# Two families of small products put into one stay on TensorE: the S5 outputs of a hybrid decoder layer

## The chip, the cores and the metric

The kernel runs on one core of a Trainium2 chip, in float32. The metric is the device time of one execution, in microseconds (us).

## What is computed

One layer of a decoder, for 256 prompt tokens and 8 samples of 4 tokens (288 tokens, 72 blocks of four). The mixer has two branches behind one large input projection; this case is about the end of the second, S5:

```python
u -> 128 groups of 16 channels, one 64-dim complex state per group
s_re, s_im = associative_scan(s5_combine, (a, b u)) + (a^t s0)      # per group
y = Re(C s) + d_skip * u
v = gelu(y) @ w_glu ; yB = v1 * sigmoid(v2)
merged = sigmoid(g_a) * yA + sigmoid(g_b) * yB
```

The kernel doesn't scan token by token. It takes blocks of four tokens: only the state at the start of each block is scanned (72 steps' worth of columns), and the four outputs of a block are the sum of

- the **Toeplitz products**: a 64 x 64 matrix for each group (4 tokens x 16 channels in, the same out; it holds C A^n B and the skip) times the block's inputs, for all 72 blocks at once, and
- the **state products**: a 64 x 64 matrix with the powers of A folded into C, once for the real and once for the imaginary part, times the states at the blocks' starts.

## The kernel before

**The stream.** TensorE works through 692 chunks of weights. A chunk is 128 x 1024 numbers in `raw`; ScalarE (ACT) rounds it to `w_hi`, VectorE (DVE) writes the remainder `w_lo`, and TensorE does 24 matmuls of 128 x 128 by 288 columns with it (`chunk`, L2092 to L2094: hi by hi, hi by lo, lo by hi). `raw`, `w_hi` and `w_lo` are rings of four chunks (`RING`), and the two roundings run three chunks ahead (`LEAD = 3`): in slot z of their programs ACT and DVE round the chunk of slot z + 3, for which ACT first waits until TensorE is through with slot z - 1. TensorE waits for `lo_ready` ahead of each chunk.

**The slots.** The stretch that matters is the loop over `SLOTS` = 84 chunks (chunk 240 + z is slot z), which all three engines have, written out by hand. Between the quarters (kt) of a chunk TensorE calls `s5_piece(z, kt)`, which puts small matmuls into the stream; each such interruption is a **stay** here. What stands where:

- slots 12 to 27 (`IN0`, `SCAN0`): matrices and inputs of the scan, among them the input products (`inputs`, L2365), 64 x 64 by 72 columns as well, on all four quarters of the array;
- slots 28 to 58 (`SCAN0` to `OUT0`): DVE runs the scan, two steps a slot (L1766, L1770, L1772), around its rounding;
- slots 38, 44, 50 and 56: the Toeplitz products of two blocks of 8 pairs of groups each (`t_products`, L2378). Pair p has two groups e = 0, 1; group e is read from partitions 64e and written to partitions 64e, so only two quarters of the array work. ACT lays the matrices out for them first (`t_block` into `tbd`) and copies the results over `u2` (`t_copy`);
- slots 59, 60, 62, 63, 65, 66, 68 and 69 (`out_slot`): the state products of one block each (`s5_out`, L2396), on four quarters. ACT copies the block's states ahead of them (`states_lay`, `states_lay_first`, into `so5`), DVE makes the matrices (`o_matrices`, into `qc` and `qc2` by turns, three operations for each of two parts) and adds the products to `u2` a slot later (`y_add`);
- `y_store` and `y_load` on GpSimd (POOL) move `u2` through a DRAM scratch, two blocks at a time, to the layout of features, and from slot 70 on `gelu_square`, `gelu_arg`, `gelu_tanh`, `gelu_out`, `v_round` and `v_remainder` make the operand of the GLU product, which begins in slot 84.

All of this waits on semaphores by count; several names share a semaphore (`SHARED`), and `reach` and `wait` add what the first user has left on it.

## Time and profile before

| | us |
|---|---|
| median of 3 runs | 2367.04 (2366.74 to 2367.44) |
| span of the profiled execution | 2365.0 |
| TensorE busy | 2358.0 (100%) |
| VectorE busy | 1654.1 (70%) |
| ScalarE busy | 1059.4 (45%) |
| Toeplitz products (L2378), 256 records in 4 stays | 8.9 |
| state products (L2396), 512 records in 8 stays | 9.8 |

The profiled execution's own time is its 2365.0 us span and some 2 us around it, by the median of the runs. The chain of waits that ended last is 99% TensorE. The trace shows a float32 matmul of the small kind as two records, each a load of 64 columns of weights and a pass of 72 columns, so 128 products are 256 records. Line numbers are those of the kernel before.

### The profile page before, as it was taken

To read this page: it belongs to the slowest core of one execution; us is meant where nothing else is said; L and a number is where in the kernel's file an instruction comes from. 1 tells how busy PE (TensorE), PEld (TensorE's weight loads), DVE (VectorE), ACT (ScalarE), POOL (GpSimd) and SP (SyncE) were. 2 spreads that over 40 slices of the span, in tenths; PEclk is the share of its full clock that TensorE was granted. 3 is DMA by queue.
4 is the path that set the end of the run, shared out by engine and by line. 5 is a ranking of instruction groups with operands and counts; after the bars stand their busy time and mean duration, and the time that the engine had idled before them with its cause. 6 is when DMAs were issued, how large, how long until landed. Compare 5 with 4: busy or idle time off the path is not lost.

```text
span 2365.0 us, 49376 instructions
## 1 busy us (share of the span) xinstructions
PE 2358.0 (100%) x19158; PEld 2305.6 (97%) x19158; DVE 1654.1 (70%) x2923; ACT 1059.4 (45%) x1567; POOL 109.2 (5%) x202
## 2 busy tenths in 40 slices
PE   9999999999999999999999999999999999999999
PEld 9999999999999999999999999999999999999998
DVE  7798988979888877798966655765555555544444
ACT  6553544535444445545643333553343334333333
POOL 1000000000000002100400000000000000000000
PEclk9999999999999999999999999999999999999999
DMA  7676766677676678465877766555655555565543
GB/s 213 203 226 203 239 197 207 215 214 237 187 222 204 219 236 232 146 185 166 249 203 199 203 194 201 178 169 158 174 161 161 170 161 165 169 200 165 169 159 117
DMA packets 546111, 453.93 MB, mean 192 GB/s; under 512 B 31184, under 2 KB 520112, under 8 KB 545408
## 3 DMA queue, kind: packets, MB, share of 16 engines
q1 hardware_dynamic: 525936, 406.23, 57.3%
q0 software_dynamic: 13392, 34.33, 4.5%
q10 hardware_dynamic: 6624, 11.18, 1.4%
q8 instruction: 109, 1.79, 0.3%
q14 instruction: 50, 0.41, 0.1%
HBM read 412.01 MB, written 38.81 MB: 191 GB/s over the span
## 4 chain that ended last, share of the span: by engine, by line
PE 99%; DVE 0%; issue 0%; ACT 0%; POOL 0%; POOLq 0%; DVEq 0%
PE acc L2092 31%; PE acc L2093 30%; PE acc L2094 30%; PE side L2079 1%; PE side L2178 1%; PE side L2230 1%; PE side L2365 0%; PE side L2102 0%; PE side L2396 0%; PE side L2378 0%; PE side L2211 0%; PE acc L2577 0%; PE side L2577 0%; PE side L2576 0%; PE acc L2576 0%; PE side L2575 0%
## 5 line engine op out<-in xcount | busy, mean ns | idle before, releaser
L1291 DVE TENSOR_TENSOR w_lo<-raw,w_hi 128x1024 fp32r<-128x1024 f32 (+2 forms) x692 | 831.0, 1208 | 508.2 <-ACT w_hi L792 503.1
L792 ACT ACTIVATE w_hi<-raw 128x1024 fp32r<-128x1024 f32 (+2 forms) x692 | 717.0, 1046 | 884.7 <-PE acc L2094 857.9
L2092 PE MATMUL acc<-h_hi,w_hi 128*128 128x288 f32 x3344 | 1000.9, 299 | 0.0
L2094 PE MATMUL acc<-h_hi,w_lo 128*128 128x288 f32 x3344 | 986.1, 295 | 0.0
L2093 PE MATMUL acc<-h_lo,w_hi 128*128 128x288 f32 x3344 | 985.2, 295 | 0.0
L2092 PEld LDWEIGHTS acc<-h_hi,w_hi 128*128 128x128 f32 x3344 | 627.9, 188 | 17.5 <-issue 15.1
L2093 PEld LDWEIGHTS acc<-h_lo,w_hi 128*128 128x128 f32 x3344 | 627.4, 188 | 2.2 <-issue 2.2
L2094 PEld LDWEIGHTS acc<-h_hi,w_lo 128*128 128x128 f32 x3344 | 627.8, 188 | 0.0
L2092 PE MATMUL acc<-f_hi,w_hi 128*128 128x288 f32 x698 | 207.0, 296 | 0.0
L2094 PE MATMUL acc<-f_hi,w_lo 128*128 128x288 f32 x698 | 205.7, 295 | 0.0
L2093 PE MATMUL acc<-f_lo,w_hi 128*128 128x288 f32 x698 | 205.4, 294 | 0.0
L2092 PE MATMUL acc<-y_hi,w_hi 128*128 128x288 f32 x512 | 155.4, 304 | 0.0
L2094 PE MATMUL acc<-v_hi,w_lo 128*128 128x288 f32 x512 | 151.8, 296 | 0.0
L2093 PE MATMUL acc<-v_lo,w_hi 128*128 128x288 f32 x512 | 151.6, 296 | 0.0
L2094 PE MATMUL acc<-y_hi,w_lo 128*128 128x288 f32 x512 | 150.9, 295 | 0.0
L2092 PE MATMUL acc<-v_hi,w_hi 128*128 128x288 f32 x512 | 150.9, 295 | 0.0
L2093 PE MATMUL acc<-y_lo,w_hi 128*128 128x288 f32 x512 | 150.7, 294 | 0.0
L2092 PEld LDWEIGHTS acc<-f_hi,w_hi 128*128 128x128 f32 x698 | 131.1, 188 | 0.0
L2094 PEld LDWEIGHTS acc<-f_hi,w_lo 128*128 128x128 f32 x698 | 131.0, 188 | 0.0
L2093 PEld LDWEIGHTS acc<-f_lo,w_hi 128*128 128x128 f32 x698 | 130.8, 187 | 0.0
L2092 PEld LDWEIGHTS acc<-y_hi,w_hi 128*128 128x128 f32 x512 | 96.2, 188 | 1.9 <-issue 1.7
L2093 PEld LDWEIGHTS acc<-y_lo,w_hi 128*128 128x128 f32 x512 | 96.1, 188 | 1.7 <-issue 1.7
(407 smaller groups left out, 2685.7 us busy)
## 6 DMA issues: line engine op xcount, KB each, us to landing
raw<-in_w_in_dram SPq DMA_DIRECT2D x512, 256.0 KB, 3.4
raw<-in_w_ffn_up_dram SPq DMA_DIRECT2D x352, 256.0 KB, 3.4
raw<-in_w_ffn_down_dram SPq DMA_DIRECT2D x160, 256.0 KB, 2.9
raw<-in_w_ssm_out_dram SPq DMA_DIRECT2D x128, 256.0 KB, 3.4
raw<-in_w_glu_dram SPq DMA_DIRECT2D x128, 256.0 KB, 3.7
h<-in_state_ssm_dram SPq DMA_DIRECT2D x32, 512.0 KB, 6.9
out_ssm_sample_dram<-h POOLq DMA_DIRECT2D x32, 512.0 KB, 3.8
raw<-in_w_out_dram SPq DMA_DIRECT2D x64, 256.0 KB, 3.2
```

The lines of the kernel that those rows point to most:

```text
L792: copy = lambda out, in_, **k: nc.scalar.activation(out, in_, ACT.Copy, **k)
L1291: tt(w_lo[:, slot, 0:n], raw[:, slot, 0:n], w_hi[:, slot, 0:n].bitcast(F32), ALU.subtract).then_inc(lo_ready, 1)
L2079: return pe.transpose(out, in_, ident[0:k, 0:k])
L2092: mm(o_, wh, xh[:, kt, :], start=first and i == 0, stop=False)
L2093: mm(o_, wh, xl[:, kt, :], start=False, stop=False)
L2094: done = mm(o_, wl, xh[:, kt, :], start=False, stop=last and i == n - 1)
L2178: last = mm(bank[r:r + 64, (j // 2) * n:(j // 2 + 1) * n], xdt[0:n, c, j * HD:(j + 1) * HD], abc[0:n, j, t0:t0 + n], **one)
L2230: last = mm(s3[32 * r:32 * r + 32, :], cm[:, b, :], h0[:, b, :], start=b < 4, stop=b >= 4)
```

## The change

The Toeplitz products leave slots 38 to 56. A stay now takes two blocks: first the Toeplitz products of both, which open the sums in the PSUM banks, then the state products of both, which add to them. There are four such stays, in slots 60, 64, 68 and 72 (`out_pair`), where there were four and eight. The Toeplitz matrix is read straight from `tt5`, whose layout is turned for it: its 64 columns now lie `PAIRS` x 4 = 256 bytes apart, where `tbd` had them side by side. Group e of pair 2r + g2 goes to half e ^ g2, so that all four quarters work.

`t_block`, `t_copy` and `y_add` are gone. ACT copies the finished sums to `u2` (`y_copy`, four copies in the slot behind a stay). `states_lay(1)` moves up to slot 59 and the later ones stand in the two slots behind a stay. There are three buffers for the state matrices (`qc3` is new); the matrices of block 2 are made in slots 48 and 51, within the scan, the others behind the stays. The rows of `u2` come out in reversed token order (`y_store` and, by the host's order of `w_glu`, the GLU product allow for that).

```diff
-def out_slot(i):
-
-    return OUT0 + i + i // 2
...
+def out_pair(z):
+
+    return (z - OUT0 - 1) // 4 if z in (OUT0 + 1, OUT0 + 5, OUT0 + 9, OUT0 + 13) else -1
...
-    tt5, at = sb("tt5", [P, DL, PAIRS, S5C], F32, used["u2"][1])
+    tt5, at = sb("tt5", [P, DL, S5C, PAIRS], F32, used["u2"][1])
...
-            def t_copy(i, h):
-
-                act.wait_ge(*reach("t_product", i * 2 + (h + 1)))
-                p0 = i * PB + 4 * h
-                copy(u2[:, p0:p0 + 4, :], ((s0, s1), (s2, s3))[i % 2][h][:, 0:4 * NK].rearrange("p (g k) -> p g k", k=NK)).then_inc(sem("t_copied"), 1)
+            def y_copy(i):
+
+                for g2 in range(2):
+                    act.wait_ge(sem("y5_product"), i * 2 + (g2 + 1))
+                    bank = ((s0, s1), (s2, s3))[i % 2][g2]
+                    v = u2[:, i * PB:i * PB + PB, :].rearrange("p (r g) k -> p g r k", g=2)[:, g2]
+                    copy(v, bank[:, 0:4 * NK].rearrange("p (g k) -> p g k", k=NK)).then_inc(sem("s5_y_copied"), 1)
...
                 if z == OUT0:
                     states_lay(0, 56)
-                if 0 <= out_block(z) < 7:
-                    states_lay(out_block(z) + 1)
+                    states_lay(1)
+                if out_pair(z - 1) >= 0:
+                    for i in (0, 1):
+                        y_copy(2 * out_pair(z - 1) + i)
+                if 0 <= out_pair(z - 1) < 3:
+                    states_lay(2 * out_pair(z - 1) + 2)
+                if 0 <= out_pair(z - 2) < 3:
+                    states_lay(2 * out_pair(z - 2) + 3)
...
-                if T0 <= z < T0 + 24:
-                    if (z - T0) % 3 == 1:
-                        t_block((z - T0) // 3)
-                    if (z - T0) % 6 == 5:
-                        for h in range(4):
-                            t_copy((z - T0) // 3 - 1 + h // 2, h % 2)
...
-                wait(dve, "y5_product", i * 2 - 2)
-                matrices(i, part, (qc, qc2)[i % 2], ct5, po5, ALU.add, ALU.subtract, "o")
-
-            def y_add(i):
-
-                dve.wait_ge(*reach("t_copied", i * 2 + 2))
...
+                if i == 2:
+                    dve.wait_ge(sem("p_product"), 16)
+                wait(dve, "y5_product", i * 2 - 4)
+                matrices(i, part, (qc, qc2, qc3)[i % 3], ct5, po5, ALU.add, ALU.subtract, "o", back=-1)
...
                 if z in (T0 + 6, T0 + 12):
                     o_matrices(1, (z - T0 - 6) // 6)
-                if out_block(z - 1) >= 0:
-                    i = out_block(z - 1)
-                    y_add(i)
-                    if i + 2 < 8:
-                        o_matrices(i + 2, 0)
-                        o_matrices(i + 2, 1)
+                if z in (T0 + 15, T0 + 18):
+                    o_matrices(2, (z - T0 - 15) // 3)
+                if out_pair(z - 1) >= 0 and 2 * out_pair(z - 1) + 3 < 8:
+                    for part in range(2):
+                        o_matrices(2 * out_pair(z - 1) + 3, part)
...
             def t_products(i):
 
-                if i == 0:
-                    pe.wait_ge(sem("p_copied"), 32)
-                pe.wait_ge(sem("tbd_ready"), i + 1)
-                wait(pe, "t_copied", i * 2 - 2)
-                for h in range(2):
-                    for p in range(4 * h, 4 * h + 4):
-                        for e in range(2):
-                            rows = slice(64 * e, 64 * e + 64)
-                            last = mm(((s0, s1), (s2, s3))[i % 2][h][rows, (p % 4) * NK:(p % 4 + 1) * NK], tbd[rows, i % 2, p, :], u2[rows, i * PB + p, :], **one)
-                    last.then_inc(sem("t_product"), 1)
...
+                banks = ((s0, s1), (s2, s3))[i % 2]
+                for r in range(4):
+                    for e in range(2):
+                        for g2 in range(2):
+                            rows, half = slice(64 * e, 64 * e + 64), 64 * (e ^ g2)
+                            pair = i * PB + 2 * r + g2
+                            last = mm(banks[g2][half:half + 64, r * NK:(r + 1) * NK], tt5[rows, :, :, pair].rearrange("p k c -> p (k c)"), u2[rows, pair, :],
+                               start=r == 0, stop=False)
+                last.then_inc(sem("t_product"), 1)
...
+            def s5_out(j):
+
+                if j == 0:
+                    pe.wait_ge(sem("p_copied"), 32)
+                    pe.wait_ge(sem("responses_shifted"), 96)
+                    pe.wait_ge(*reach("first_laid", 1))
+                pe.wait_ge(*reach("states_laid", 2 * j + 2))
+                pe.wait_ge(*reach("o_matrices", 4 * j + 4))
+                wait(pe, "s5_y_copied", 4 * j)
+                t_products(2 * j)
+                t_products(2 * j + 1)
+                state_products(2 * j)
+                state_products(2 * j + 1)
```

TensorE's order at its first stay behind the scan, which was in slot 59 (the last row is the beginning of slot 59's last quarter). Here is before:

```order
L2092 MATMUL acc<-h_hi,w_hi 128x288
L2093 MATMUL acc<-h_lo,w_hi 128x288
L2094 MATMUL acc<-h_hi,w_lo 128x288
L2396 MATMUL side<-so_108,qc 64x72 x32
L2092 MATMUL acc<-h_hi,w_hi 128x288
```

Of the changed kernel, the same place in slot 60, 24 rows of chunk work later; `tt_115` is `tt5`, `so_108` is `so5`, `qc_107` is `qc2`:

```order
L2081 MATMUL acc<-h_hi,w_lo 128x288
L2363 MATMUL side<-u_112,tt_115 64x72 x32
L2376 MATMUL side<-so_108,qc 64x72 x32
L2376 MATMUL side<-so_108,qc_107 64x72 x32
L2079 MATMUL acc<-h_hi,w_hi 128x288
```

The first stay has moved by one slot and holds three times as many products, all behind the waits that the state products have; the rows of L2378 in slots 38 to 56 are gone.

DVE's order within the scan, in slots 48 and 49 (`scr` and `st` are the scan's). Before:

```order
L1291 TENSOR_TENSOR w_lo<-raw,w_hi 128x1024
L1770 TENSOR_TENSOR scr_122<-scr_122 128x128
L1772 TENSOR_TENSOR st_120<-st_120,scr_122 128x128
L1766 TENSOR_TENSOR scr_122<-st_120,a4t 128x256
L1770 TENSOR_TENSOR scr_122<-scr_122 128x128
L1772 TENSOR_TENSOR st_120<-st_120,scr_122 128x128
L1766 TENSOR_TENSOR scr_122<-st_120,a4t 128x256
L1291 TENSOR_TENSOR w_lo<-raw,w_hi 128x1024
```

And of the changed kernel, where `qc_128` is `qc3`:

```order
L1283 TENSOR_TENSOR w_lo<-raw,w_hi 128x1024
L1755 TENSOR_TENSOR scr_122<-scr_122 128x128
L1757 TENSOR_TENSOR st_120<-st_120,scr_122 128x128
L1751 TENSOR_TENSOR scr_122<-st_120,a4t 128x256
L1755 TENSOR_TENSOR scr_122<-scr_122 128x128
L1757 TENSOR_TENSOR st_120<-st_120,scr_122 128x128
L1704 TENSOR_TENSOR tm_110<-ct_117,po_124 128x512
L1705 TENSOR_TENSOR tm_110<-ct_117,po_124 128x512
L1710 TENSOR_TENSOR qc_128<-tm_110 128x512
L1751 TENSOR_TENSOR scr_122<-st_120,a4t 128x256
L1283 TENSOR_TENSOR w_lo<-raw,w_hi 128x1024
```

One part of block 2's matrices, three operations, now stands between two steps of the scan, and the second part the same way in slot 51.

ACT's order around the end of the scan, from slot 58. Before:

```order
L792 ACTIVATE so_108<-st_120 128x16x56
L792 ACTIVATE w_hi<-raw 128x1024
L792 ACTIVATE so_108<-st_120 128x16x16
L792 ACTIVATE so_108<-st_120 128x1152
L792 ACTIVATE w_hi<-raw 128x1024
L792 ACTIVATE so_108<-st_120 128x1152
```

Of the changed kernel:

```order
L789 ACTIVATE so_108<-st_120 128x16x56
L789 ACTIVATE w_hi<-raw 128x1024
L789 ACTIVATE so_108<-st_120 128x16x16
L789 ACTIVATE so_108<-st_120 128x1152
L789 ACTIVATE w_hi<-raw 128x1024
L1001 ACTIVATE gth<-acc 128x288 x2
L1003 DMA mix_scratch<-gth 128x576
L789 ACTIVATE w_hi<-raw 128x1024
L789 ACTIVATE u_112<-side 128x4x72 x4
L789 ACTIVATE so_108<-st_120 128x1152
```

Up to slot 59 the same copies stand in the same order, but the first stay now waits for the second of slot 59's two, which is block 1's; the copy of block 2's states has gone behind the first stay's results.

## Rows read from the trace of the kernel before

**Rows 1.** The page's busy times: us (share of the span) x instructions.

```profile
PE 2358.0 (100%) x19158; PEld 2305.6 (97%) x19158; DVE 1654.1 (70%) x2923; ACT 1059.4 (45%) x1567; POOL 109.2 (5%) x202
```

**Rows 2.** TensorE by line and form: busy us, mean ns of one | idle before.

```profile
L2396 PE MATMUL side<-so,qc 64*64 64x72 f32 x512 | 9.8, 226 | 0.3 <-issue 0.3
```

**Rows 3.** Timeline, TensorE, first Toeplitz stay: start us, us, instruction.

```profile
1026.81 0.30 PE L2094 MATMUL acc<-h_hi,w_lo 128*128 128x288 f32 x1
1027.04 2.22 PE L2378 MATMUL side<-u,tbd 64*64 64x72 f32 x64
...
1029.42 0.30 PE L2093 MATMUL acc<-h_lo,w_hi 128*128 128x288 f32 x1
```

**Rows 4.** Timeline, TensorE, first state stay, next chunk, last state stay.

```profile
1104.70 0.30 PE L2094 MATMUL acc<-h_hi,w_lo 128*128 128x288 f32 x1
1104.92 1.23 PE L2396 MATMUL side<-so,qc 64*64 64x72 f32 x64
...
1106.32 0.30 PE L2093 MATMUL acc<-h_lo,w_hi 128*128 128x288 f32 x1
...
1106.99 0.29 PE L2092 MATMUL acc<-h_hi,w_hi 128*128 128x288 f32 x1
...
1146.64 1.23 PE L2396 MATMUL side<-so,qc 64*64 64x72 f32 x64 [0.28 <-issue]
```

**Rows 5.** Timeline, TensorE, one stay of input products.

```profile
941.49 0.98 PE L2365 MATMUL side<-u,pw 64*64 64x72 f32 x48
```

**Rows 6.** Windows, 90 us of the scan: PE, PEld, DVE, ACT, POOL busy (x records), clock.

```profile
1000.00:1090.00 90.00, 90.00 (x819) 89.27 (x818) 85.01 (x190) 42.52 (x82) 5.66 (x7) 1.00 0.61 182
```

**Rows 7.** Timeline, VectorE: roundings of slots 33, 38, 39, 40, 58; scan's end.

```profile
1013.10 1.22 DVE L1291 TENSOR_TENSOR w_lo<-raw,w_hi 128x1024 fp32r<-128x1024 f32 x1
...
1029.27 1.22 DVE L1291 TENSOR_TENSOR w_lo<-raw,w_hi 128x1024 fp32r<-128x1024 f32 x1
...
1033.04 1.23 DVE L1291 TENSOR_TENSOR w_lo<-raw,w_hi 128x1024 fp32r<-128x1024 f32 x1 [0.46 <-ACT w_hi L792]
...
1038.21 1.22 DVE L1291 TENSOR_TENSOR w_lo<-raw,w_hi 128x1024 fp32r<-128x1024 f32 x1
...
1100.66 1.22 DVE L1291 TENSOR_TENSOR w_lo<-raw,w_hi 128x1024 fp32r<-128x1024 f32 x1
...
1103.22 0.29 DVE L1772 TENSOR_TENSOR st<-st,scr 128x128 f32<-128x128 f32 x1
```

**Rows 8.** Timeline, ScalarE: roundings of slots 34, 35, 60; copies of states.

```profile
1013.66 1.06 ACT L792 ACTIVATE w_hi<-raw 128x1024 fp32r<-128x1024 f32 x1 [2.12 <-PE acc L2094]
...
1016.85 1.06 ACT L792 ACTIVATE w_hi<-raw 128x1024 fp32r<-128x1024 f32 x1 [1.33 <-PE acc L2094]
...
1103.66 2.83 ACT L792 ACTIVATE so<-st 128x256 f32<-128x256 f32 x2
1107.25 1.06 ACT L792 ACTIVATE w_hi<-raw 128x1024 fp32r<-128x1024 f32 x1 [0.75 <-PE acc L2094]
```

**Rows 9.** Windows, TensorE: window, us, busy (x records), granted clock, DMA.

```profile
2.00:4.00 2.00, 1.97 (x9) 1.00 0.90 250
6.00:8.00 2.00, 2.00 (x20) 1.00 1.03 430
...
2364.00:2365.00 1.00, 0.00 (x0) 0.59 0.15 50
```

**Rows 10.** Timeline, TensorE: its last matmuls.

```profile
2360.82 0.65 PE L2518 MATMUL side<-fW,ident 128*128 128x288 f32 x2
```

**Rows 11.** ScalarE by line and form, 985 to 1195 us: busy us, mean ns.

```profile
L792 ACT ACTIVATE w_hi<-raw 128x1024 fp32r<-128x1024 f32 x59 | 62.5, 1060 | 77.2 <-PE acc L2094 76.6 <-ACT gth L1004 0.5
L792 ACT ACTIVATE so<-st 128x1152 f32<-128x1152 f32 x7 | 16.2, 2315 | 0.0
```

**Rows 12.** Timeline, GpSimd: store and load of the last quarter of y.

```profile
1154.18 4.48 POOL L763 DMA_DIRECT2D y_scratch<-u  x8
...
1166.54 1.34 POOL L773 DMA_DIRECT2D yt<-y_scratch  x2 [0.83 <-issue]
```

More of the change, by code:

```diff
@@ L83 @@
 FIN0 = OUT0 + 17
-def out_slot(i):
-    return OUT0 + i + i // 2
-def out_block(z):
-    return {out_slot(i): i for i in range(8)}.get(z, -1)
+def out_pair(z):
+    return (z - OUT0 - 1) // 4 if z in (OUT0 + 1, OUT0 + 5, OUT0 + 9, OUT0 + 13) else -1
 def gelu_at(z):
@@ L312, in build @@
     yt5, _ = sb("yt5", [P, KT, T], F32, used["u2"][0])
-    gsq, at = sb("gsq", [P, 2, T], F32, used["tt5"][0])
-    gar, at = sb("gar", [P, 2, T], F32, at)
-    assert at <= used["tt5"][1]
+    gsq, at = sb("gsq", [P, 2, T], F32, used["qc3"][0])
+    assert at <= used["qc3"][1]
+    gar, at = sb("gar", [P, 2, T], F32, used["tm5"][0])
+    assert at <= used["tm5"][1]
     v_hi, at = sb("v_hi", [P, KT, T], F32R, used["st5"][0])
@@ L1703, in _, with matrices @@
                 s5_parameters(t)
-            def matrices(i, part, bd, src, pows, re_sub, im_rev, s, n=DL):
+            def matrices(i, part, bd, src, pows, re_sub, im_rev, s, n=DL, back=1):
                 block = slice(i * PB, i * PB + PB)
                 xr, xi = [bc(src[:, k, block, :], n, 2) for k in range(2)]
-                qr, qi = [bc(pows[:, k, 0:n, block].rearrange("x j p -> x p j"), S5C, 3) for k in range(2)]
+                qr, qi = [bc(pows[:, k, 0:n, block][:, ::back].rearrange("x j p -> x p j"), S5C, 3) for k in range(2)]
                 v = [tm5[:, k, 0:PB * n * S5C].rearrange("x (p j c) -> x p j c", p=PB, j=n) for k in range(2)]
@@ L1843, in _ @@
                     o_matrices(1, (z - T0 - 6) // 6)
-                if out_block(z - 1) >= 0:
-                    i = out_block(z - 1)
-                    y_add(i)
-                    if i + 2 < 8:
-                        o_matrices(i + 2, 0)
-                        o_matrices(i + 2, 1)
+                if z in (T0 + 15, T0 + 18):
[3 more added lines that the diff above has]
+                        o_matrices(2 * out_pair(z - 1) + 3, part)
+                for part in range(2):
+                    if out_pair(z - 2 - part) >= 0 and 2 * out_pair(z - 2 - part) + 4 < 8:
+                        o_matrices(2 * out_pair(z - 2 - part) + 4, part)
                 if gelu_at(z - 1) >= 0:
@@ L2415, in s5_piece @@
                         inputs(7, 1)
[L2416 to L2422 removed]
+                if out_pair(z) >= 0 and kt == 2:
+                    s5_out(out_pair(z))
             pe.wait_ge(sem("y_split"), 32)
@@ L2674 @@
     quarters = [2 * (i // 4) + i % 2 + 8 * (i % 4 // 2) for i in range(KT)]
-    given['w_glu'] = given['w_glu'].reshape(1, KT, P, 2 * D_MODEL)[:, quarters].reshape(1, D_MODEL, 2 * D_MODEL)
+    by_tile = given['w_glu'].reshape(1, KT, 4, 2, S5C, 2 * D_MODEL)[:, quarters]
+    by_tile = _np.stack([by_tile[:, i, :, ::-1] if i % 4 // 2 else by_tile[:, i] for i in range(KT)], axis=1)
+    given['w_glu'] = by_tile.reshape(1, D_MODEL, 2 * D_MODEL)
     arrays, a, o = {}, {}, {}
```

58 lines of the change are left out of this document (18 added, 40 removed).

## The prediction

> **What bounds the kernel now.** First the page's busy times: TensorE is busy for 2358.0 us of a 2365.0 us span [rows 1]. Then its waits: in 90 us of the stretch of this change there is none [rows 6], and among the small products one of 0.3 us [rows 2], ahead of the last state stay [rows 4]. So all that leaves TensorE is gained in full, as long as nobody else becomes late. That is the second question, and it goes to the engine whose share of the whole (70%) hides where it stands: in 90 us of the scan VectorE is busy for 85.01 [rows 6], and its timeline is a gapless row of short dependent operations. The pace of that row against the pace of TensorE decides this case.
>
> **What TensorE sheds.** A Toeplitz stay: from the last matmul ahead (1026.81) to the second behind (1029.42) are 2.61 us [rows 3]. Without a stay two matmul steps would lie there; 24 matmuls take 3.19 us (two roundings of ScalarE, each released by a finished chunk, are 3.19 apart [rows 8]), so a step is 0.133 and the stay costs 2.61 - 0.27 = 2.34. A state stay costs 1106.32 - 1104.70 = 1.62, less 0.27: 1.35 [rows 4]. Before: 4 x 2.34 + 8 x 1.35 = 20.2 us, and the 0.3 of waiting.
>
> After: 128 Toeplitz products (256 records) and 256 state products (512) in 4 stays, 192 records each. The pace of the state products: 64 records run 1.23 us to the end of the last, which itself takes 0.226 [rows 2], so (1.23 - 0.23) / 63 = 0.016 a record [rows 4]. The Toeplitz products of before, on two quarters: (2.22 - 0.22) / 63 = 0.032 [rows 3]. The input products, of the same size, on four quarters and in the same order of rows and halves as the new Toeplitz products: (0.98 - 0.22) / 47 = 0.016 [rows 5]. Four records in 0.064 us on four quarters, two in 0.064 on two: the quarters work side by side. I take 0.016 for the new Toeplitz products too, since the two rows nearest in form have it; the upper bounds follow with the rivals. A stay is then 1.35 + 128 x 0.016 = 3.40, four are 13.6. **TensorE sheds 20.2 + 0.3 - 13.6 = 6.9 us.** If nothing else moved, that would be the gain.
>
> **What VectorE gets in the scan.** Its period per slot is one rounding and two scan steps: from 1013.10 (slot 33) to 1029.27 (slot 38) are 5 periods of 3.234 us [rows 7]. TensorE's slot without a stay is 3.187 (24 steps). So VectorE is slower than TensorE by 0.047 us a slot all through the scan, and what let it keep up were the Toeplitz stays, 2.34 us each, in which TensorE stood aside. It shows: the first slot behind the first of them is where VectorE had to wait (0.46 at 1033.04 [rows 7]). The change takes all four away and adds work: one part of `o_matrices` stretches a period to 1038.21 - 1033.04 = 5.17, so it costs 1.94, and there are now four of them in the scan (slots 39, 45, 48, 51) where there were two.
>
> Nothing makes VectorE wait any more from slot 33 on, so slot 58 rounds at 1013.10 + 25 x 3.234 + 4 x 1.94 = 1101.7, and the scan ends as long behind it as before (1103.22 + 0.29 - 1100.66 = 2.85 [rows 7]): at **1104.6**. Before it was 1103.5, with 9.4 us of Toeplitz stays in TensorE's program to cover it.
>
> TensorE: a chunk begins 0.26 us ahead of the ScalarE rounding that it releases (1106.99 and 1107.25 [rows 4, 8]), so slot 34 begins at 1013.66 - 0.26 = 1013.40. Unhindered, slot 60 would begin 26 slots on, at 1096.3, and its three quarters would be through at 1098.7. Two waits stand against that:
>
> - The remainders. Chunk 52 is rounded in slot 49, at 1013.10 + 16 x 3.234 + 3 x 1.94 + 1.22 = 1071.9; TensorE wants it at 1013.40 + 18 x 3.187 = 1070.8. From there on VectorE sets the pace. Chunk 60 is ready at 1101.7 - 3.2 + 1.2 = 1099.7, so slot 60 begins 3.4 us late and comes to its stay at 1102.1.
> - The states. The stay in slot 60 wants block 0's and block 1's states, and the last of the scan goes into both. ScalarE copied them in 2.83 us from 0.15 after the scan's end [rows 7, 8]; after, that is 1104.6 + 2.98 = **1107.6**. TensorE stands for 5.5 us. In the queue behind ScalarE's wait are the roundings from slot 60 on, which TensorE doesn't want before slot 63. Before, TensorE needed only block 0's states at this point, a slot earlier, and came late enough.
>
> Together 8.9 us of new waits. In TensorE's time: the stay begins at 1107.6, is through at 1111.0; before, the same point of slot 60 was 1106.99 + 2.39 + 1.35 = 1110.7, so the change is 0.3 behind. Later stays: before 6 x 1.35 + 0.3 = 8.4, after 3 x 3.40 = 10.2, 1.8 more. **Net 2.0 us slower.**
>
> **The clock.** TensorE's last matmul ends at 2361.47 [rows 10], and in the last microsecond of the span the granted clock is 0.59 on average [rows 9]: it had fallen to the lower level, 1.2 GHz, by about 2364.2, 2.7 us after the last work. The new wait is twice as long, behind a dense stretch. At the kernel's start the records come at half pace, 9 in two microseconds against 20 from 6 us on [rows 9]: after a pause TensorE ran at the lower level for some 3.4 us of work. The same behind the first stay's wait costs half of that: 1.7 us. I count it in: 2.0 + 1.7 = **3.7 us slower**.
>
> **What costs nothing, and why.** Leaving: ScalarE's `t_block` and `t_copy` (it is busy for 42.52 of 90 us there [rows 6]). Coming: 16 `y_copy` in place of 16 copies of the same 288 columns, and two copies of states in the two slots behind each stay. Behind the first stay ScalarE has 1.06 + 4 x 0.4 + 2.3 = 5.0 us in a slot of 3.2 and 3.4 in the next [rows 11]; it falls 2 us behind and has them back before the next stay, whose states are then laid. The lead of the roundings is three slots, 9.6 us, less the 2.3 that the two take. VectorE loses eight `y_add` and gets the matrices over two or three slots each. The last two blocks are finished in slot 72, not 69: y is copied at about 1163, and store and load took 1166.54 + 1.34 + about 5 - 1154.18 = 19 us [rows 12], so it is there at 1182, against 1180.6 when ScalarE comes to it in slot 79. A wait of some 1.6 us, inside the lead; without that cover it would cost just this. `skip_added` and the copies into `tt5` keep their sizes; the latter fall in slots 13 to 27, where VectorE has idle time in every slot.
>
> **Rivals.**
>
> *Slower weight loads (the other side: clearly slower).* The new Toeplitz matrices are read at a step of 256 bytes. No row of TensorE has such a read. ScalarE has: 1152 states with a step of 512 bytes took 2315 ns, 2.01 each, 1024 weights side by side 1060, 1.04 each [rows 11]. If a load of 64 columns, which by its share of 64 in 64 + 72 columns takes 30 ns of the 64 that a quarter needs, takes twice as long, four records take 30 ns more: 7.5 x 256 = 1.9 us. If it takes ScalarE's 2.01 ns a column, 129 in place of 30: 99 / 4 x 256 = 6.3 us. Net 3.9 to 8.3 with the full clock, 5.6 to 10.0 with the fall. Against it speaks only that nothing says TensorE reads as ScalarE does. From 1.0 us on it would make the loss measurable.
>
> The Trainium skill has this as a rule (SBUF — State Buffer, "Specifications (TRN2)"): SBUF has lines of 16 bytes, full bandwidth needs at least two hits on a line, and each step to a new line pays. It gives no price, and read for TensorE it would make this rival the likeliest case. ScalarE's two rows [rows 11] agree with it; for TensorE no row shows it.
>
> *The clock stays up.* The 5.5 us are a sum of small terms, and the only fall in the trace came behind a sparse stretch. If this wait brings none, net 2.0: 2369.0.
>
> *The cover holds.* If VectorE's period shrinks when TensorE reads less, or the first stay's waits are already met, the 6.9 us are gained: 2360.1. Against it: the five periods of 3.234 include the first Toeplitz stay (1027.04 to 1029.2 [rows 3]), and the period at 1013.10 wasn't waiting for anything either.
>
> **How the numbers follow.** The profiled execution took its span of 2365.0 and some 2 us around it; I add to the median, 2367.04. Forecast: 2367.04 + 3.7 = 2370.7 us, chance 0.32. Clock stays up: 2369.0, 0.18. Slower loads: 2371 to 2377, 0.42, of which 0.34 lie over 2371.8. Gain: 2360.1, 0.05. The rest, 0.03, is scattered. 0.2% of the time, about what a measurement can tell from no change, is 4.7 us: faster 0.05, same 0.60, slower 0.35. The range leaves out the gain and the dearest loads with a fallen clock: 2368.0 to 2375.4.
>
> **What would show it.** Right: no L2378 stays, four stays in slots 60, 64, 68, 72; VectorE without a gap from slot 33 to the scan's end at about 1104.6; TensorE's chunks waiting for `w_lo` from slot 52 on, at most 2 us at once, then about 5.5 us ahead of the first stay; a granted clock under 1 behind it; a later stay of 3.4 us. A later stay of 3.9 to 5.0 means slow loads. No wait ahead of slot 60's stay would prove the argument on VectorE wrong, and so would a scan that ends before 1103.

## Result and profile after

The changed kernel took 2379.76 us (median of 4 runs, 2378.83 to 2383.74) beside 2367.16 us for the kernel before on the same chip (4 runs): ratio 1.0057, 95% interval 1.0045 to 1.0068. It is slower by 12.6 us. The forecast was 2370.7, its range ended at 2375.4, and the likeliest sign was "same". The profiled execution has a span of 2377.1 us against 2365.0.

The page of the kernel after, engines and the chain that ended last (compare [rows 1]; the chain was 99% TensorE, now VectorE is in it):

```profile
PE 2359.8 (99%) x19158; PEld 2308.7 (97%) x19158; DVE 1649.3 (69%) x2907; ACT 1050.4 (44%) x1535; POOL 109.2 (5%) x202
...
PE 95%; DVE 5%; issue 0%; ACT 0%; POOL 0%; POOLq 0%; ACTq 0%; DVEq 0%
```

TensorE's waits in 985 to 1210 us of the kernel after (engine, line, what it waited for: us in total, times, longest). In the same place before there was one of 0.3 [rows 4]:

```profile
PE side L2363 <- ACT so L789: 5.1, 1, 5.1
PE acc L2079 <- DVE w_lo L1283: 2.8, 2, 1.7
PE acc L2079 <- issue: 2.7, 1, 2.7
```

The first two are the waits of the prediction. The third, "issue", is time in which TensorE stood and no engine's work is shown as what it waited for. Nothing in the prediction answers to it.

The first stay (slot 60) in the timelines of VectorE, ScalarE and TensorE, and TensorE's granted clock around it (columns of the windows: length, busy time of PE, PEld, DVE, ACT and POOL with their instructions, clock, DMA share, GB/s):

```profile
1105.01 0.29 DVE L1757 TENSOR_TENSOR st<-st,scr 128x128 f32<-128x128 f32 x1
```

```profile
1105.34 2.70 ACT L789 ACTIVATE so<-st 128x256 f32<-128x256 f32 x2 [6.28 <-DVE st L1757]
```

```profile
1108.30 2.63 PE L2363 MATMUL side<-u,tt 64*64 64x72 f32 x64 [5.09 <-ACT so L789]
1110.63 3.61 PE L2376 MATMUL side<-so,qc 64*64 64x72 f32 x128
```

```profile
1106.00:1107.00 1.00, 0.00 (x0) 0.00 (x0) 0.44 (x1) 1.00 (x1) 0.00 (x0) 0.86 0.69 240
1107.00:1108.00 1.00, 0.00 (x0) 0.00 (x0) 0.00 (x0) 1.00 (x2) 0.00 (x0) 0.50 0.27 54
...
1113.00:1114.00 1.00, 1.00 (x57) 1.00 (x52) 0.00 (x0) 0.00 (x0) 0.00 (x0) 0.73 0.52 178
1114.00:1116.00 2.00, 2.00 (x30) 1.92 (x20) 0.00 (x0) 0.67 (x1) 0.00 (x0) 1.00 0.00 0
```

The scan ends at 1105.30 (on this trace, whose chunks already start 0.8 us later at the kernel's beginning), ScalarE copies the states, TensorE starts when they are there. Its clock falls to the lower level while it waits and is back at the higher one towards 1113.5; 128 records of the state products take 3.61 us here and 2.18 in a later stay.

The last stay (slot 72), with the chunk around it (compare [rows 3] and [rows 4]):

```profile
1161.78 0.29 PE L2081 MATMUL acc<-h_hi,w_lo 128*128 128x288 f32 x1
1162.01 2.58 PE L2363 MATMUL side<-u,tt 64*64 64x72 f32 x64
1164.40 2.18 PE L2376 MATMUL side<-so,qc 64*64 64x72 f32 x128
...
1166.75 0.29 PE L2080 MATMUL acc<-h_lo,w_hi 128*128 128x288 f32 x1
1166.88 0.29 PE L2081 MATMUL acc<-h_hi,w_lo 128*128 128x288 f32 x1
1169.84 0.40 PE L2079 MATMUL acc<-h_hi,w_hi 128*128 128x288 f32 x1 [2.66 <-issue]
```

Measured as in the prediction, a later stay costs 1166.75 - 1161.78 - 0.27 = 4.70 us, not 3.40. The state products run as forecast (128 records in some 2.2 us). The Toeplitz products don't: 64 records take 1164.40 - 1162.01 = 2.39 us, where 16 ns each would be 1.02. And 2.96 us, less one step of 0.13, are lost three matmuls behind the stay.

**The ledger.** Comparing the starts of all chunks in the two traces, slot by slot, gives the whole difference of the spans (12.1):

| | forecast, us | measured, us |
|---|---|---|
| start of the kernel, ahead of all chunks | 0 | +0.8 |
| stays of before gone (4 of 2.34, 8 of 1.35, wait 0.3) | -20.5 | -20.6 |
| four new stays at the full clock | +13.6 | +18.8 |
| waits for `w_lo`, slots 51 to 59 | +3.4 | +3.5 |
| wait for the states, slot 60 | +5.5 | +5.1 |
| lower clock in slot 60 | +1.7 | +1.5 |
| gap behind the last stay | 0 | +2.9 |
| sum | +3.7 | +12.0 |

Two rows are off: the stays by 5.2, and the gap. The runs go after both, and after what the waits are worth.

### The profile page after: what moved, and what is told of

The parts are those of the page before. It is cut to its first block, busy times and chain, and to the rows that moved or that the text cites. A ratio compares the mean times of both kernels' runs of the same rounds, so it can differ in the third digit from the quotient of the medians.

```text
span 2377.1 us, 49310 instructions
## 1 busy us (share of the span) xinstructions
PE 2359.8 (99%) x19158; PEld 2308.7 (97%) x19158; DVE 1649.3 (69%) x2907; ACT 1050.4 (44%) x1535; POOL 109.2 (5%) x202
## 4 chain that ended last, share of the span: by engine, by line
PE 95%; DVE 5%; issue 0%; ACT 0%; POOL 0%; POOLq 0%; ACTq 0%; DVEq 0%
PE acc L2079 29%; PE acc L2080 28%; PE acc L2081 28%; DVE w_lo L1283 1%; PE side L2066 1%; DVE scr L1751 1%; PE side L2165 1%; DVE st L1757 1%; DVE scr L1755 1%; PE side L2217 1%; PE side L2089 0%; PE side L2352 0%; PE side L2363 0%; PE side L2376 0%; PE side L2198 0%
```

## Experiments

### The step of the weights

Contiguous weights in an otherwise unchanged kernel. Only the address is changed, so that the Toeplitz products multiply by wrong numbers:

```diff
-                            last = mm(banks[g2][half:half + 64, r * NK:(r + 1) * NK], tt5[rows, :, :, pair].rearrange("p k c -> p (k c)"), u2[rows, pair, :],
+                            last = mm(banks[g2][half:half + 64, r * NK:(r + 1) * NK], tt5[rows, :, :, :].rearrange("p k c q -> p (k c q)")[:, pair * 64:pair * 64 + 64], u2[rows, pair, :],
```

> The changed kernel, but the Toeplitz products read 64 weights side by side (columns 64p to 64p + 63 of tt5) in place of 64 at a step of 256 bytes; these are other numbers, so y is not the layer's. Theory (the step makes the loads slow): a record of the Toeplitz products takes 16 ns in place of 36, a stay 3.4 us in place of 4.7, the kernel 4 x 1.3 = 5.2 us less, about 2374.5. Rival (both row halves of the array write into one bank): pace stays 36 ns, time stays 2379.8. Open: whether the 2.7 us without an instruction, seen in the last slot of stays, stays.

Measured: 2378.57 us (5 runs, 2374.78 to 2380.97), 1.0043 (1.0029 to 1.0058). TensorE's last stay in the timeline:

```profile
1158.26 1.23 PE L2363 MATMUL side<-u,tt 64*64 64x72 f32 x64
1159.31 2.18 PE L2376 MATMUL side<-so,qc 64*64 64x72 f32 x128
...
1167.64 0.61 PE L2079 MATMUL acc<-h_hi,w_hi 128*128 128x288 f32 x1 [5.55 <-issue]
```

The 64 records take 1.05 us: the pace of 16 ns that the prediction took is there, and it was the step that broke it. Yet of the 5.2 us that were expected the medians show 1.2, less than the runs of either kernel scatter, and the profiled execution shows none: its span is 2379.2. By the starts of the chunks the first three stays gave back 0.6, 1.3 and 1.3 us, but the last one cost 4.3 more. It was 1.3 shorter, the gap behind it grew by 2.9 (from 2.7 to 5.5 of idle time), and the chunks behind it took 2.7 longer at the lower clock. The faster stay had the longer gap.

Different steps in one kernel show where the price begins. Again the Toeplitz products multiply by wrong numbers.

```diff
+STEP = (64, 64, 1, 2, 4, 8, 16, 32)
...
-                            last = mm(banks[g2][half:half + 64, r * NK:(r + 1) * NK], tt5[rows, :, :, pair].rearrange("p k c -> p (k c)"), u2[rows, pair, :],
+                            last = mm(banks[g2][half:half + 64, r * NK:(r + 1) * NK], tt5[rows, :, :, :].rearrange("p k c q -> p (k c q)")[:, (pair % 8) * (8 if STEP[i] < 64 else 1):][:, 0:63 * STEP[i] + 1:STEP[i]], u2[rows, pair, :],
```

> The changed kernel with another step of the Toeplitz weights for each block of pairs: 256 bytes for blocks 0 and 1, then 4, 8, 16, 32, 64 and 128 bytes for blocks 2 to 7; other numbers are read, so y is not the layer's. Theory (lines of 16 bytes, two hits wanted): 16 ns a record for 4 and 8 bytes, about 36 from 16 bytes on, all alike. Rival (the step must be long, as in a clash of memory banks): 16 ns up to 64 or 128 bytes and 36 for 256 alone.

Measured: 2378.61 us (one run). The stays of blocks 2 and 3 (steps of 4 and 8 bytes), 4 and 5 (16 and 32), and 6 and 7 (64 and 128), Toeplitz products above and state products below:

```profile
1125.46 1.23 PE L2364 MATMUL side<-u,tt 64*64 64x72 f32 x64
1126.51 2.18 PE L2377 MATMUL side<-so,qc 64*64 64x72 f32 x128
...
1141.56 2.16 PE L2364 MATMUL side<-u,tt 64*64 64x72 f32 x64
1143.54 2.19 PE L2377 MATMUL side<-so,qc 64*64 64x72 f32 x128
...
1159.14 2.03 PE L2364 MATMUL side<-u,tt 64*64 64x72 f32 x64
1160.99 2.18 PE L2377 MATMUL side<-so,qc 64*64 64x72 f32 x128
```

From the first Toeplitz product to the first state product: 1.05, 1.98 and 1.85 us; with 256 bytes, in the kernel after, 2.39. Counted as in the prediction (the time to the end of the last record less that record's own, over 63), a record of 64 columns costs 16 ns with steps of up to 8 bytes, 28 to 30 from 16 bytes on, and 36 at 256. So neither expectation was met whole: the price begins at 16 bytes, but it isn't the same from there on. Its beginning is the rule of the Trainium skill (SBUF — State Buffer, "Specifications (TRN2)") that the prediction weighed, a line of 16 bytes that wants two hits, with the price that the page doesn't give. That 256 bytes cost more than 128 is beyond the rule; why, no run tells. Nor does this price follow TensorE's clock: with 256 bytes the 64 records take 2.63 us in the first stay, at the lower level, and 2.58 in the last, side by side 2.20 and 1.23 (the first stay of the run before).

### What the waits are worth

The matrices of block 2 made behind the scan instead of in it:

```diff
-                if z in (T0 + 15, T0 + 18):
-                    o_matrices(2, (z - T0 - 15) // 3)
+                if z in (OUT0, OUT0 + 1):
+                    o_matrices(2, z - OUT0)
```

> The changed kernel with block 2's matrices (six operations of VectorE, 3.9 us) made in slots 59 and 60 and not within the scan. Theory (VectorE paces the scan): the scan ends 3.9 us earlier, TensorE's waits for w_lo (1.2 + 2.0 + some 0.2 us) vanish, the wait ahead of the first stay is about 4.6 us in place of 5.1, and the kernel takes 3.9 us less, about 2375.9. Rival (the waits come from late weights or from the clock): the waits for w_lo stay and the time with them.

Measured: 2375.46 us (6 runs, 2374.06 to 2378.49, all below those of the changed kernel), 1.0036 (1.0024 to 1.0049). TensorE's waits in 985 to 1210:

```profile
PE side L2363 <- ACT so L789: 4.9, 1, 4.9
PE acc L2079 <- issue: 3.3, 1, 3.3
```

No wait for `w_lo`: the 3.5 us are gone from the starts of the chunks, and the medians differ by 4.3, near the 3.9 that two parts of 1.94 us on VectorE's row make. The argument on VectorE's pace is confirmed. (The profiled execution is only 1.1 us shorter, since its gap was longer and the clock fell behind it.)

The Toeplitz products ahead of the wait for the states:

```diff
-                    pe.wait_ge(*reach("first_laid", 1))
-                pe.wait_ge(*reach("states_laid", 2 * j + 2))
-                pe.wait_ge(*reach("o_matrices", 4 * j + 4))
                 wait(pe, "s5_y_copied", 4 * j)
                 t_products(2 * j)
                 t_products(2 * j + 1)
+                if j == 0:
+                    pe.wait_ge(*reach("first_laid", 1))
+                pe.wait_ge(*reach("states_laid", 2 * j + 2))
+                pe.wait_ge(*reach("o_matrices", 4 * j + 4))
```

> The changed kernel with the Toeplitz products of each stay ahead of the waits for the states and the matrices. Theory (5 us of standing, then a fallen clock): the 2.3 us of Toeplitz products of the first stay fit into the gap, the wait behind them is about 2.8 us; 2.4 us less, and if the clock then holds, 1.5 more: 2375.9 to 2377.4. Rival (the clock falls all the same, since the gap plus the sparse products count as a pause): 2377.4 at best.

Measured: 2378.26 us (4 runs, 2377.62 to 2381.1), 1.0046 (1.0029 to 1.0063).

```profile
1103.35 2.59 PE L2363 MATMUL side<-u,tt 64*64 64x72 f32 x64
1108.37 4.12 PE L2376 MATMUL side<-so,qc 64*64 64x72 f32 x128 [2.44 <-issue]
```

The wait is halved (2.4; it is that for the states, whose copies end at 1108.2), but the clock falls in it all the same (lower level from 1107.0 to 1113.8) and the state products pay for it: 4.12 us for 2.18. By the chunks' starts the first stay costs 1.3 us less, not the 2.4 of the Toeplitz products. The medians say 1.5, which the scatter of the runs doesn't tell from nothing.

### The gap that no engine explains

The gap was in each of the five kernels so far with two blocks a stay, always behind the last stay, with 2.7 to 5.5 us of "issue", and not in the kernel before. The first idea was the length of the stay. Here each block has its own stay; both still wait for the states and matrices of the pair.

```diff
-            def s5_out(j):
+            def s5_out(j, m):
...
-                t_products(2 * j)
-                t_products(2 * j + 1)
-                state_products(2 * j)
-                state_products(2 * j + 1)
+                t_products(i)
+                state_products(i)
...
+                    for m in range(2):
+                        if out_pair(z - m) >= 0 and kt == 2:
+                            s5_out(out_pair(z - m), m)
```

> The changed kernel with each two-block stay cut in two: block 2j's Toeplitz and state products in slot 60+4j as before, block 2j+1's in slot 61+4j, so 192 PE instructions at a time in place of 384. Nothing else differs. Theory (the 2.9 to 5.8 us in which TensorE stood behind the last stay is its instruction stream, drained by 384 short instructions in a row): in slots 72 to 75 no gap over 0.5 us with issue as its cause, stays of about 2.35 us each, span 3 us below the changed kernel's 2377.1, that is 2373 to 2375; the wait ahead of the first stay stays at about 5.1 because block 0 and 1 are still waited for in the same order by ScalarE (block 0's alone may be some 1.2 shorter). Rival (the stall hangs on where TensorE stands in the program or on the y stores and loads of that time): the gap of 3 us or more is still there about 1167, and the time stays at 2377 to 2380.

Measured: 2380.59 us, 1.0056 (1.0041 to 1.0071). The gap is gone: the stays of slots 72 and 73 end in chunks without any idle time. But the kernel isn't faster. One of its stays:

```profile
1165.18 0.29 PE L2081 MATMUL acc<-h_hi,w_lo 128*128 128x288 f32 x1
1165.41 1.41 PE L2363 MATMUL side<-u,tt 64*64 64x72 f32 x32
1166.90 1.23 PE L2376 MATMUL side<-so,qc 64*64 64x72 f32 x64
...
1168.30 0.29 PE L2080 MATMUL acc<-h_lo,w_hi 128*128 128x288 f32 x1
```

It costs 1168.30 - 1165.18 - 0.27 = 2.85 us, two of them 5.70, and the two-block stay 4.70. One us more for each of four pairs takes back what the gap gave. About half of it is inside the stays: the first state product starts 0.40 us behind the last Toeplitz product, on which it depends, in the two-block stay 0.12. The rest is one more entry and exit. I had expected 3 us of gain and not counted that.

The two-block stay with weights side by side and the scan relieved. ScalarE copies the matrices into `tbd` as before the change, block 2's matrices have left the scan, and the Toeplitz products stand ahead of the wait for the states (the diff shows the products alone):

```diff
-                            last = mm(banks[g2][half:half + 64, r * NK:(r + 1) * NK], tt5[rows, :, :, pair].rearrange("p k c -> p (k c)"), u2[rows, pair, :],
+                            last = mm(banks[g2][half:half + 64, r * NK:(r + 1) * NK], tbd[rows, i % 2, 2 * r + g2, :], u2[rows, pair, :],
...
+                wait(pe, "s5_y_copied", 4 * j)
+                pe.wait_ge(sem("tbd_ready"), 2 * j + 2)
+                t_products(2 * j)
+                t_products(2 * j + 1)
```

> The changed kernel's four two-block stays, but the Toeplitz matrices side by side (copied by ScalarE into a buffer of two blocks, one copy a block, as before the change), no third buffer for the matrices of the state products and so no matrices of block 2 in the scan, and the Toeplitz products of a stay ahead of its waits for states. Theory: later stays at 3.3 us in place of 4.7 (4.2 us less in three of them and the first), no waits for w_lo (2.8), a gap ahead of the first stay of 2 to 3 us; but the 384 instructions in a row are still there and take less time, so the stall about 1167 remains with 3 to 6 us. Together 2368 to 2372. Rival (the stall came from the waits that the scan's matrices caused, or from late lead): no stall, 2363 to 2366.

Measured: 2373.49 us (6 runs, 2370.8 to 2375.34), 1.0026 (1.0014 to 1.0038), above the 2368 to 2372 expected.

```profile
1099.01 1.23 PE L2369 MATMUL side<-u,tbd 64*64 64x72 f32 x64
1103.83 4.12 PE L2382 MATMUL side<-so,qc 64*64 64x72 f32 x128 [3.59 <-issue]
...
1163.36 0.47 PE L2086 MATMUL acc<-h_lo,w_hi 128*128 128x288 f32 x1 [5.04 <-issue]
```

The gap stays, 5.0 us, and again the shorter stay has the longer gap. (The first gap is the wait for the states; ScalarE's copies end there.) The later stays cost 3.56 each. With this kernel the rival, a gap from the waits that the scan's matrices caused, is out: no chunk waits for `w_lo` here.

**What TensorE's program shows.** The trace has a DMA queue for instructions. From the page of the kernel after:

```profile
q8 instruction: 109, 1.79, 0.3%
```

109 packets, 16.4 KB each (16384 bytes each in the records). With 64 bytes an instruction that is 256 instructions in a packet. (The Trainium skill, Perfetto Trace Analysis, "The 4-stage abstract model", gives these 64 bytes.) TensorE's instructions can be counted in the trace: two for each matmul record (the load of its weights and the product) and one for each wait or register operation of its sequencer. A slot of 24 matmuls has 48, so 256 are 5.33 slots or 17.0 us, and between 1001.7 and 1068.6 us one packet comes every 16.7.

By this count 20417 instructions lie ahead of the gap. In all six kernels with two blocks a stay it is 20416 or 20417, although TensorE then stands at different instructions: behind three matmuls in four of them, behind two where one wait more stands ahead (Toeplitz products first), behind one where four more do (weights side by side). Now pair the packets, in the order in which they came, with the places that lie multiples of 256 from there. It comes out with none left over, from the first packet on: in all twelve kernels each of the first 70 packets starts between 3.0 us ahead of its place and 3.4 behind it, in the middle some 1 us ahead. These places are called boundaries here. (The expectation below puts the same stop at 20992. That number counts four instructions for each of the 288 transposes ahead of it, of which the trace shows two, and its places in a stay are two lower. Neither changes a distance between two stops.) The boundaries in the stays of the kernel after:

```
boundary  place in its stay   passed at   packet starts at   next boundary passed at
18369     76 (slot 60)        1109.7      1109.5             1113.6
18625     332                 1113.6      1113.7             1127.3
18881     10 (slot 64)        1127.3      1126.1             1130.6
19137     266                 1130.6      1134.3             1140.8
19393     138 behind it       1140.8      1139.3             1147.5
19649     200 (slot 68)       1147.5      1150.8             1153.8
19905     72 behind it        1153.8      1155.0             1164.4
20161     134 (slot 72)       1164.4      1167.4             1166.9: stands until 1169.84
20417     6 behind it         1166.9      1170.9             1186.8
```

The packet that goes with boundary 20161 should bring the block from 20417 on. In the chunk stream there are 17 us for that. Here the 256 instructions last 2.5 us, the packet starts 3.0 us after the boundary and takes 1.1, and 1.3 later TensorE goes on. In slot 64 the 256 behind 18881 lie almost as close (3.3 us, and 2.0 and 2.2 in the two runs with weights side by side), but that packet had started 1 us ahead of its boundary, in the chunks before the stay, and TensorE didn't stop. So it isn't only that the stay is long, but where in the block it lies, and that can be shifted.

The other traces say the same. In each of the six kernels TensorE goes on 1.3 to 1.5 us after the end of the packet that brings the block; three short stops of 0.2 to 0.5 us, behind the stay of slot 68 in the runs with different steps, with block 2's matrices late and with the Toeplitz products first, end 1.2 to 1.5 us after one. Where each block has its own stay, the 256 instructions between two boundaries last 6.1 us or more in the stays of the split kernel, and there is no gap.

The changed kernel with a shorter warm-up, which shifts all that follows by 72 instructions and nothing else near the stays:

```diff
-WARM = 36
+WARM = 18
```

> The changed kernel with 18 of its 36 warm-up matmuls at the very start left out (they compute nothing that is used). That takes 72 instructions out of TensorE's stream ahead of everything else, and shifts where the 16384-byte fetches of 256 instructions fall. In the traces so far TensorE stood exactly at the instruction that begins a new block of 256 in the last stay (number 20992, four behind the stay's end), with the block boundary ahead of it 132 instructions into the same stay; in the other stays a boundary lay 74, 8 and 198 instructions in. With 72 fewer, the boundaries lie 146, 80, 14 and 204 instructions in. Theory (a fetch arrives some 5.5 to 8 us after it is asked for, a little ahead of the boundary, and the block behind it must not be used up by then: only a boundary some 30 to 170 instructions into a two-block stay stalls it): the gap in slot 72 about 1167 is gone, and one of 2 to 4 us stands inside the stay of slot 64, 336 instructions in, about 1130; the first stay, slower by its clock, shows at most a small one. The sum of the time changes little; the start may cost 0 to 3 us more. Rival (a debt that builds up over four stays, or the y stores of that time): the gap is still in slot 72 and none is in slot 64.

Measured: 2384.13 us, 1.0072 (1.0054 to 1.0091; two runs). TensorE's stays of slots 64 and 72:

```profile
1129.61 2.58 PE L2363 MATMUL side<-u,tt 64*64 64x72 f32 x64
1131.99 1.85 PE L2376 MATMUL side<-so,qc 64*64 64x72 f32 x105
1137.54 0.60 PE L2376 MATMUL side<-so,qc 64*64 64x72 f32 x23 [3.71 <-issue]
...
1170.00 2.57 PE L2363 MATMUL side<-u,tt 64*64 64x72 f32 x64
1172.39 2.17 PE L2376 MATMUL side<-so,qc 64*64 64x72 f32 x128
```

The gap left slot 72 and now splits the stay of slot 64, behind 64 + 105 records, that is 338 instructions: the boundary that lay 266 in, and the 72 that are gone ahead of it. By the count it is 19137, and 20417 - 19137 is 5 x 256. The packet starts 3.9 us behind its boundary, ends at 1136.09, and TensorE goes on 1.4 us later. The debt over four stays and the stores of y are out. The gap is the fetch of TensorE's own instructions. The span rose by 5.0 us, more than expected: 3.5 of it at the start (TensorE now stands 4.0 us for VectorE ahead of the transposes of the input; the first chunk begins 1.5 later and takes 5.0 us for 3.0, with the clock at the lower level from 12.3 us on), 1.2 in a longer gap and 1.3 from the clock that fell behind it, less 1.1 in the first stay.

### A version without the three losses

One block a stay in slots 61 to 71, the Toeplitz matrices side by side in a small buffer (as before the change), no matrices of block 2 in the scan, the Toeplitz products ahead of the wait for the states:

```diff
-    return (z - OUT0 - 1) // 4 if z in (OUT0 + 1, OUT0 + 5, OUT0 + 9, OUT0 + 13) else -1
+    return {OUT0 + 2 + i + i // 2: i for i in range(8)}.get(z, -1)
...
-                matrices(i, part, (qc, qc2, qc3)[i % 3], ct5, po5, ALU.add, ALU.subtract, "o", back=-1)
+                matrices(i, part, (qc, qc2)[i % 2], ct5, po5, ALU.add, ALU.subtract, "o", back=-1)
...
+                wait(pe, "s5_y_copied", 2 * i - 2)
+                pe.wait_ge(sem("tbd_ready"), i + 1)
+                t_products(i)
+                if i == 0:
+                    pe.wait_ge(*reach("first_laid", 1))
+                pe.wait_ge(*reach("states_laid", i + 1))
+                pe.wait_ge(*reach("o_matrices", 2 * i + 2))
+                state_products(i)
```

> One accumulation of Toeplitz and state products and one copy of y, as in the changed kernel, but one block a stay in eight stays (slots 61, 62, 64, 65, 67, 68, 70, 71), Toeplitz matrices side by side in a buffer of two blocks that ScalarE fills, no block-2 matrices in the scan, a block's Toeplitz products ahead of its wait for states. Theory: TensorE no longer waits for w_lo nor ahead of the first stay (its states are laid by about 1107 and slot 61's third quarter ends later), the clock stays at 1.00 and no fetch stall comes; eight stays of 1.35 + 0.5 = 1.9 us in place of 20.2 us in all: about 5 us faster than the kernel before, 2361 to 2363. Rival (the gap in TensorE's instructions comes with any 192 in a row, or VectorE's pace without the four Toeplitz stays makes TensorE wait anyhow): 2365 to 2369.

Measured: 2365.13 us (11 runs, 2364.26 to 2365.96) beside 2366.84 (23 runs, 2366.52 to 2367.9), 0.9991 (0.9982 to 1.0000), span 2362.7, clock 1.00 up to the last work, no wait for VectorE or ScalarE, no gap. All three losses are gone. It gained 1.7 us, not 5, since a stay costs 2.26 and not 1.9:

```profile
1130.10 0.29 PE L2080 MATMUL acc<-h_hi,w_lo 128*128 128x288 f32 x1
1130.32 0.73 PE L2362 MATMUL side<-u,tbd 64*64 64x72 f32 x32
1131.23 1.23 PE L2375 MATMUL side<-so,qc 64*64 64x72 f32 x64 [0.18 <-PE side L2362]
...
1132.63 0.29 PE L2079 MATMUL acc<-h_lo,w_hi 128*128 128x288 f32 x1
```

The same, a slot earlier, prices the wait at the first stay:

```diff
-    return {OUT0 + 2 + i + i // 2: i for i in range(8)}.get(z, -1)
+    return {OUT0 + 1 + i + i // 2: i for i in range(8)}.get(z, -1)
```

> The kernel that has one block a stay in slots 61 to 71, with every stay one slot earlier (60, 61, 63, 64, 66, 67, 69, 70). It tells what the first stay's place costs. Theory: TensorE comes to the first stay's state products about 3 us before the states are laid and stands there 1.5 to 3 us; if the clock falls behind that gap, another 1 to 2 us. 2363 to 2366, so 2 to 4 us over the one that begins in slot 61. Rival (VectorE's scan ends earlier when TensorE has no gap, or the gap is too short for the clock): within 1 us of the other.

Measured: 2368.23 us, 1.0005 (0.9996 to 1.0014), 3.1 us over the other. TensorE's timeline, and the clock:

```profile
1101.64 1.98 PE L2375 MATMUL side<-so,qc 64*64 64x72 f32 x64 [2.01 <-ACT so L788]
```

```profile
1102.00:1105.00 3.00, 3.00 (x63) 2.86 (x54) 0.34 (x1) 3.00 (x4) 0.00 (x0) 0.50 0.64 195
```

2.0 us of waiting, and 0.75 us on the state products (1.98 for 1.23), the rest on the chunk behind them at the lower clock. One slot's delay buys both.

Last, a stay's own inner wait: the Toeplitz products of the next block behind the state products of this one. (The first stay has those of blocks 0 and 1, ahead of its state products.)

```diff
                 state_products(i)
+                if 1 <= i < 7:
+                    wait(pe, "s5_y_copied", 2 * i)
+                    pe.wait_ge(sem("tbd_ready"), i + 2)
+                    t_products(i + 1)
```

> The kernel with one block a stay from slot 61 on (2362.7 span, 2365.1), but block i+1's Toeplitz products stand behind block i's state products in stay i, so that no state product waits for Toeplitz products just ahead of it (1.4 us in eight waits there). The first stay holds the Toeplitz products of blocks 0 and 1 and the states of 0, the last only states. Theory (each stay's cost was 1.54 of work, 0.49 of its ends and 0.23 of that wait): stays add 2.03 in place of 2.26 us, together 1.5 to 1.8 less: span 2361.0 to 2361.3, 2363.4 to 2363.8 beside 2366.9 for the kernel before, ratio 0.9986. Rival (the copies that ScalarE must now have made earlier, of y and of the next Toeplitz matrices, are late in the adjacent slots): waits of 0.5 to 1 us for them in slots 62, 65 and 68, and no gain.

Measured: 2362.11 us (11 runs, 2361.26 to 2363.33) beside 2366.86, ratio 0.9979 (0.9970 to 0.9988). The same stay in its timeline, and all of TensorE's waits from 985 to 1210:

```profile
1129.21 0.29 PE L2080 MATMUL acc<-h_hi,w_lo 128*128 128x288 f32 x1
1129.44 1.23 PE L2375 MATMUL side<-so,qc 64*64 64x72 f32 x64
1130.49 0.68 PE L2362 MATMUL side<-u,tbd 64*64 64x72 f32 x32
...
1131.34 0.29 PE L2079 MATMUL acc<-h_lo,w_hi 128*128 128x288 f32 x1
```

```profile
PE side L2362 <- ACT tbd L788: 0.2, 1, 0.2
```

A stay costs 1131.34 - 1129.21 - 0.27 = 1.86 us, 0.40 less than in the version before it; I had expected 0.23, and 2363.4 to 2363.8 in all. I had taken the idle time alone (0.18 above). The starts show more: there the first state product starts 0.40 us behind the last Toeplitz product, here the next block's first Toeplitz product 0.04 behind the last state product, on which it doesn't depend. The version is 4.8 us faster than the kernel before and 17.7 faster than the changed one.

## The prediction, step by step

- **What bounds the kernel, and the scan's pace: right.** TensorE is nearly always busy, and each us that it stands is lost. VectorE's row without a gap set the scan's end: forecast 1104.6, measured 1105.3 less the 0.8 of the later start. The waits for `w_lo` began in slot 52 and cost 3.5 for the 3.4 forecast. The states came in 1107.6, measured 1108.3 less 0.8. The wait was 5.1 for 5.5. The run with block 2's matrices behind the scan confirms the mechanism, not only the numbers.
- **The clock: right**, 1.5 us for 1.7. The run with the Toeplitz products first adds that half the wait brings a fall too, and a dearer one (2.8 us by the chunks' starts): the stepped Toeplitz products, which cost no more at the lower level, no longer stand in the slow stretch.
- **What is removed: right**, 20.6 for 20.5.
- **The Toeplitz products at 16 ns a record: wrong, by 5.2 us.** I took the pace from "the two rows nearest in form", which were near in tile shape and order, but had their weights side by side, and the disputed property was the step. The rows that had that property were ScalarE's [rows 11], and their bounds, 1.9 to 6.3 us, held the 5.2. The rival "slower weight loads" was the case that came, with a later stay of 4.70 where its sign was 3.9 to 5.0, and it had the larger chance (0.42 for 0.32); the forecast stood on a case with less. By it, with the fallen clock, the time would have been up to 2377, and the range was cut at 2375.4, leaving out just the dearest loads, near which it came.
- **The gap of 2.9 us: in no case.** The prediction put this term at nothing without a reason: it asked of each wait which engine releases it, and this one has no releaser among the engines. The profile of before had the queue of instruction packets and their rhythm; the density of a stay in instructions per us, some 84 (384 in 4.6 us) for 15 in the chunks, was never set against it. In which stay the gap came, if in any, hung on where the boundaries fell, and that was chance.
- **"What costs nothing": held.** TensorE waits neither for ScalarE's roundings nor for y. ScalarE waited 4.2 us for y where 1.6 were worked out, inside the lead.
- **The rival "the cover holds"** was rightly small: the waits came as worked out.

Added up with the measured pace alone, the prediction's sum would be 2370.7 + 5.2 = 2375.9. The other 3.9 to the median are the gap (2.9) and the 0.8 at the start, with differences of a few tenths. What moved the start was not looked into; it isn't the same in each trace (first chunk at 15.8 to 16.8, the shortened warm-up aside).

## To carry to other kernels

Choose the row that bounds an unseen operation by the property in dispute (here the step of the weights), not by shape; when the rival that follows from it has the larger chance, it is the forecast. When small matmuls are gathered into denser stays, price the stay's entry and exit (0.3 us here: a state stay of before cost 1.35, and its 64 records make 1.02 of it), the delay of a product behind the one on which it depends (0.40 us against 0.04), and the instructions it takes per us against what the instruction queue brings; that last loss depends on the place in the program, and an edit far ahead can move or remove it. An engine that stands aside gives time to the one behind it: before such a pause is removed, see who lived on it.

## What the hardware showed

- Small float32 products (64 columns of weights, 72 moving), four quarters of the array at work: 16 ns a record with steps of 4 and 8 bytes between the weights, 28 to 30 from 16 to 128 bytes, 36 at 256. At the lower clock the 256-byte ones took the same (2.63 us for 64 records beside 2.58), those side by side 2.20 for 1.23.
- TensorE's instructions come in packets of 16384 bytes, one for each 256 instructions passed. While a loop of it ran again (from 1254 to 1408 us in the kernel after, 395 instructions a turn) none came. Where TensorE passed the 256 ahead of a boundary in 2.2 to 2.5 us and the packet to come had started 3.0 to 5.5 us behind the boundary before, it stood for 2.7 to 5.5 us, until 1.3 to 1.5 us after the packet's end, and the stop moved with the boundary. Where the packet had started ahead of the boundary, 256 passed in 2.0 us without a stop. Why packets start late inside a stay isn't settled.
- Waits of 2.0, 2.4, 3.6 and 5.1 us ahead of or in the first stay each brought TensorE to its lower clock, at a price of 1.3 to 2.8 us, which doesn't follow the length of the wait. The gap of 2.7 us in the kernel after brought no fall; those of 3.3 us and more did. A fall needs no wait: in the profiled execution of the last version the clock is at the lower level from 2347.5 to 2354.3, and from 2340 to 2348 TensorE was busy for 7.98 of 8 us.
